# Norms of the second stream placed inside other projections, queries and keys reordered, bank halves reduced first

## What is computed

```python
# layer 2 (pool), for both streams; layer 3 (attention), queries of the latent stream only
mod = silu(c) @ ada_w[i] + ada_b[i]            # sh1, sc1, g1, sh2, sc2, g2; with c_ctx for the context
a = modulate(rms_norm(h, norm_g[i, 0]), sh1, sc1)
y = pool_mix(a, pool_w, pool_scale)            # layer 2: windowed means, then a 1024 x 256 grouped product
h = h + g1 * y
m = modulate(rms_norm(h, norm_g[i, 1]), sh2, sc2)
h = h + g2 * (square(relu(m @ mlp_w1[i])) @ mlp_w2[i])   # hidden width 4096
# layer 3
q, k, v = qkv(a_latent); kc, vc = qkv(a_context)         # 8 query heads, 4 key/value heads of 128
q, k = axial_rope(head_norm(q)), axial_rope(head_norm(k)); kc = head_norm(kc)
y_latent = attention(q, [kc, k], [vc, v]) @ w_o          # then the MLP and a last norm
```

## Time and profile before

| | us |
|---|---|
| median of 3 runs | 1587.86 |
| the profiled execution | 1588.41 |
| its span in the profile | 1585.9 |
| PE busy | 1490.0 |
| DVE busy | 1113.0 |
| ACT busy | 760.0 |

### The profile page before, as it was taken

The page is one execution under the profiler, slowest core; times in us unless marked ns, Lnnn a source line. Parts: engine busy times, 40 slices in busy tenths (PEclk is TensorE's granted clock), DMA queues, the critical chain, the costliest instruction groups (busy, mean ns, idle before and its releaser), DMA issues.

```text
span 1585.9 us, 21196 instructions
## 1 busy us (share of the span) xinstructions
PE 1490.0 (94%) x8517; PEld 1202.0 (76%) x8517; DVE 1113.0 (70%) x1682; ACT 760.0 (48%) x1184; POOL 0.2 (0%) x4
## 2 busy tenths in 40 slices
PE   5999899999999799999999999899999998899997
PEld 3767778888787568888778878688787776778786
DVE  3566758998769868998676555867767685465656
ACT  3334544444544445344465544555545534455543
POOL 0000000000000000000000000000000000000000
PEclk9999999999999899999999999899999999999999
DMA  9993158888565757776647555486674740245452
GB/s 361 343 320 136 54 186 292 293 286 304 206 239 183 243 186 260 266 245 239 213 151 274 186 186 186 161 302 233 248 255 146 269 140 27 79 133 178 172 189 86
DMA packets 167913, 335.22 MB, mean 211 GB/s; under 512 B 8192, under 2 KB 109192, under 8 KB 167816
## 3 DMA queue, kind: packets, MB, share of 16 engines
q1 hardware_dynamic: 140992, 235.09, 43.8%
q10 hardware_dynamic: 26824, 98.79, 16.8%
HBM read 332.81 MB, written 1.05 MB: 211 GB/s over the span
## 4 chain that ended last, share of the span: by engine, by line
PE 59%; DVE 25%; ACT 8%; DMA 4%; issue 4%; ACTq 0%; SPq 0%; DVEq 0%
PE ps L1860 11%; PE ps L1861 11%; PE ps L1862 11%; PE ps L1929 11%; DVE wlo L1138 9%; PE ps L1930 5%; ACT whi L659 4%; DVE hbuf L1160 3%; DMA ring<-in_ada_w_dram 3%; ACT hbuf L679 2%; PE ps L1791 1%; DVE res L1226 1%; DVE work L1224 1%; PE ps L2024 1%; PE ps L2101 1%
## 5 line engine op out<-in xcount | busy, mean ns | idle before, releaser
L1138 DVE TENSOR_TENSOR wlo<-wraw,whi 128x1024 fp32r<-128x1024 f32 (+1 forms) x420 | 493.2, 1216 | 202.9 <-ACT whi L659 202.3
L659 ACT ACTIVATE whi<-wraw 128x1024 fp32r<-128x1024 f32 (+1 forms) x420 | 418.3, 1044 | 227.0 <-PE ps L1862 139.1
L1929 PE MATMUL ps<-hT,whi 128*128 128x512 f32 x1472 | 519.4, 398 | 2.7 <-DVE hT L1281 2.7
L1930 PE MATMUL ps<-hT,wlo 128*128 128x256 f32 x1472 | 411.1, 279 | 0.0
L1929 PEld LDWEIGHTS ps<-hT,whi 128*128 128x128 f32 x1472 | 276.5, 188 | 74.0 <-DVE hT L1281 4.3
L1930 PEld LDWEIGHTS ps<-hT,wlo 128*128 128x128 f32 x1472 | 277.7, 189 | 0.0
L1860 PE MATMUL ps<-whi,act_hi 128*128 128x512 f32 x560 | 219.6, 392 | 9.0 <-DVE wlo L1138 9.0
L1862 PE MATMUL ps<-whi,act_lo 128*128 128x512 f32 x560 | 218.0, 389 | 0.0
L1861 PE MATMUL ps<-wlo,act_hi 128*128 128x512 f32 x560 | 218.0, 389 | 0.0
L1860 PE MATMUL ps<-whi,hT 128*128 128x512 f32 (+2 forms) x416 | 161.6, 388 | 4.6 <-DVE hT L1281 3.9
L1861 PE MATMUL ps<-wlo,hT 128*128 128x512 f32 (+2 forms) x416 | 158.7, 382 | 0.0
(11 more groups left out here) (230 smaller groups left out, 1398.8 us busy)
## 6 DMA issues: line engine op xcount, KB each, us to landing
wraw<-in_mlp_w_dram SPq DMA_DIRECT2D x96, 1024.0 KB, 5.3
ring<-in_ada_w_dram ACTq DMA_DIRECT2D x64, 1024.0 KB, 7.0
work<-in_ada_w_dram ACTq DMA_DIRECT2D x28, 1024.0 KB, 7.6
wraw<-in_ffn_w_gate_dram SPq DMA_DIRECT2D x22, 1024.0 KB, 5.5
wraw<-in_ffn_w_up_dram SPq DMA_DIRECT2D x22, 1024.0 KB, 6.8
wraw<-in_ffn_w_down_dram SPq DMA_DIRECT2D x22, 1024.0 KB, 5.0
wraw<-in_diff_w_in_dram SPq DMA_DIRECT2D x12, 1024.0 KB, 5.2
wraw<-in_attn_w_qkv_dram SPq DMA_DIRECT2D x12, 1024.0 KB, 5.0
```

What stands on the lines that cost most here:

```text
L659: nc.scalar.activation(whi[:, u % 2, part], raw_view(u)[:, part], ACT.Copy).then_inc(hi_ready, 1)
L1138: nc.vector.tensor_tensor(wlo[:, u % 2, part], raw_view(u)[:, part], whi[:, u % 2, part].bitcast(F32), ALU.subtract).then_inc(lo_ready, 1)
L1929: mm(ps[:, bank, :], whi[:, u % 2, c0:c0 + P], hT[:, :, k, :], start=(k == 0), stop=False, skip_group_check=True)
L1930: ins = mm(ps[:, bank, 0:S], wlo[:, u % 2, c0:c0 + P], hT_hi[:, k, :], start=False, stop=(k == KT - 1), skip_group_check=True)
```

## The change

It has five parts.

1. In DVE's stream, hidden_out(i) comes ahead of split_unit(i + 2) in every up and pair stream.
2. Norm 6 (the context's pooling norm) runs beside down20, and norm 8, which is now the latent stream's attention norm, beside down21: ACT takes squares at units 4 and 5, scales at 7 and does columns at 10 and 13, DVE does rows at 6 and columns at 10 and 14, PE its products after units 9 and 12. The columns go to other memory (spent), the pool matrices are loaded at unit 6. pool1's products then come straight after down20; the pool's gate products come after them, in banks of their own, and nine idle products stand after each pool in the place of the vector units.
3. The order of the last projections is q3, kvl, kvc. Norm 9 is the context's; its rows run beside q3, its transposes after kvl's second unit, and it is placed into hT as kvl's units let go of it. The head norms follow in the order q3, kvl, kvc, and columns(3, 1) move from attention into q3.
4. Vectors 18, 19 (both streams), 22 and 23 join 20 and 21 in SUMMED: 20 adds in up20, 12 in down20, and the same in up21 and down21. The vector units in the gaps go.
5. A product into a bank waits for that bank alone (bank_emptied); IDLE_NORM loses two entries, IDLE_HEADS[3] goes from 46 to 20.

The core of the diff:

```diff
-        IDLE_NORM = {1: 7, 2: 6, 4: 2, 8: 6, 9: 2, 10: 5}
+        IDLE_NORM = {1: 7, 2: 6, 4: 2, 10: 5}
-        IDLE_HEADS = {1: 5, 3: 46}
+        IDLE_HEADS = {1: 5, 3: 20}
+        IDLE_POOL = 9
...
-        seg("kvc", "row", [QKV[:, :, 1024:2048]], 4)
         seg("q3", "row", [QKV[:, :, 0:1024]], 4)
         seg("kvl", "row", [QKV[:, :, 1024:2048]], 4)
+        seg("kvc", "row", [QKV[:, :, 1024:2048]], 4)
...
-        VECTOR_AT = list(range(20)) + [22, 23, 20, 21]
+        VECTOR_AT = list(range(20)) + [21, 22, 20, 23]
...
+        LATE = ("up20", "down20", "up21", "down21")
+        SUM_SPANS = [(("up0", "down0"), (6, 7, 8), slots(1, 22, 24)), (("up0", "down0"), (9,), slots(22, 28, 8)),
+                     (("up1", "down1"), (15, 16), slots(1, 27, 32)), (LATE, (18, 19), slots(1, 16, 20) + slots(18, 28, 12)),
+                     (LATE, (20, 21, 22, 23), slots(33, 48, 20) + slots(50, 60, 12))]
...
         NORMS = [(0, 0, 0), (0, 0, 1), (0, 1, 0), (0, 1, 1), (0, 2, 0), (0, 2, 1), (1, 2, 0), (1, 2, 1),
-                 (1, 3, 0), (0, 3, 0), (0, 3, 1)]
+                 (0, 3, 0), (1, 3, 0), (0, 3, 1)]
+        BESIDE_DOWN = (6, 8)
...
+            def norm_beside_down(i):
+                if i == 2:
+                    root_table()
+                if i in (4, 5):
+                    norm_squares((i - 4,))
+                if i == 7:
+                    norm_scale()
+                if i == 10:
+                    norm_columns((1,))
+                if i == 13:
+                    norm_columns((3,))
...
                 for i in range(s_["count"]):
-                    if i < s_["count"] - 2:
-                        split_unit(s_["base"] + i + 2)
-                    if i == s_["count"] - 2 or i == s_["count"] - 1 and not hold_last:
+                    hidden_out(s_, i)
+                    if i < s_["count"] - 1 or not hold_last:
                         split_unit(s_["base"] + i + 2)
-                    hidden_out(s_, i)
                     row_adds(name, i)
...
+                else:
+                    held_split("down20")
+                    pool_gate(1, POOL_GATE_BANKS)
                 residual(s_)
                 norm()
                 split_unit(by_name[f"pool{s_}"]["base"] + 2)
-                stream(f"up2{s_}", beside=lambda i: vector_out(19) if s_ == 1 and i == 1 else columns(3, 0) if s_ == 1 and i == 3 else None)
-                stream(f"down2{s_}", hold_last=True)
+                stream(f"up2{s_}", beside=lambda i: columns(3, 0) if s_ == 1 and i == 5 else None)
+                stream(f"down2{s_}", hold_last=True, beside=norm_beside_down)
                 residual(s_)
...
+            row_segment("q3", heads=other_rows)
+            panel_rows(q3, 0, 1024)
+            held_split("q3")
+            row_segment("kvl", heads=other_columns)
+            panel_rows(kvl, 0, 1024)
+            norm_place(3)
+            held_split("kvl")
+            heads3(1, (3,))
+            row_segment("kvc", heads=lambda i: heads3(2, range(i, min(i + 1, 3))))
+            panel_rows(kvc, 0, 1024)
             heads3(2, (3,))
+            heads3(0, range(4))
...
+            def norm_beside_down(i):
+                if i == 9:
+                    norm((0, 1, 2))
+                if i == 12:
+                    norm((3,))
...
-                if strm == 0:
-                    vector_units(18, 0, 2)
-                else:
-                    vector_units(19, 2, 4)
+                if strm == 1:
+                    gate(POOL_GATE_BANKS)
+                idle_products(T_BANKS[6][2], IDLE_POOL)
                 gate()
                 norm()
-                up_segment(f"up2{strm}", beside=lambda i: columns(3, 0, 20) if strm == 1 and i == 2 else None)
-                down_segment(f"down2{strm}")
-
-            vector_units(22, 0, 4)
-            norm()
+                up_segment(f"up2{strm}", beside=lambda i: columns(3, 0, 20) if strm == 1 and i == 4 else None)
+                down_segment(f"down2{strm}", beside=norm_beside_down)
+
+            row_segment("q3", beside=lambda i: columns(3, 1, 24) if i == 2 else None)
+            row_segment("kvl", beside=lambda i: norm() if i == 1 else None)
+            fed[0] = (sem("hT_ready"), len(HT_STEPS) * BESIDE_ROWS, HT_STEPS)
             row_segment("kvc")
-            vector_units(23, 0, 2)
-            norm()
-            row_segment("q3")
-            row_segment("kvl")
-            vector_units(23, 2, 4)
             gate()
             idle_products(IDLE_BANK, IDLE_HEADS[3])
-            columns(3, 1, 24)
```

More of the change, by code:

```diff
@@ L435, in build @@
         PANEL_SEGS = ["in0_2", "in0_0", "in0_1", "out0", "down0", "in1_0", "in1_1", "in1_2", "out1", "down1",
-                      "pool0", "down20", "pool1", "down21", "kvc", "q3", "kvl", "out3", "down3"]
+                      "pool0", "down20", "pool1", "down21", "q3", "kvl", "kvc", "out3", "down3"]
         panel_end = [by_name[n_]["base"] + by_name[n_]["count"] for n_ in PANEL_SEGS]
@@ L698, in stream @@
                         ring_fill(fill_to)
+                    if beside is not None:
+                        beside(i)
                     if s_["kind"] == "down" and i == s_["count"] - 4:
@@ L746, in norm_rows @@
                 junk = full.rearrange("p (q a) n -> p q (a n)", q=4)
-                for t in range(TT):
+                for t in tiles:
                     for h in range(2):
@@ L1298, in norm_columns, with pool_gate @@
                     low(slice(6, 8))
+            def pool_gate(s_, banks):
+                dve.wait_ge(sem("pool_landed"), 32 * (s_ + 1))
+                for h in range(2):
+                    dve.wait_ge(gate_psum, 2 * (4 + 2 * s_) + h + 1)
+                    nc.vector.tensor_tensor(gate_b[:, 512 * h:512 * h + 512], ps[:, banks[h], :], wk(2048 + 512 * h, 512), ALU.mult).then_inc(sem("pool_gate"), 1)
             def norm():
@@ L1724, in heads3, with other_rows, other_columns @@
                     rotate(rv, acos, asin, [z[:, 0:nh * 256] for z in rot3], 32)
-            for n, (name, rows) in enumerate((("q3", q3), ("kvl", kvl))):
-                row_segment(name, heads=lambda i: heads3(n, range(i, min(i + 1, 3))))
-                panel_rows(rows, 0, 1024)
-                if name == "q3":
-                    held_split(name)
-                heads3(n, (3,))
-            heads3(2, range(3))
-            vector_out(23)
+            def other_rows(i):
+                if i == 2:
+                    norm_rows()
+                if i == 3:
+                    columns(3, 1)
+            def other_columns(i):
+                if i == 1:
+                    norm_modulate()
+                if i == 2:
+                    norm_place(0)
+                    norm_place(1)
+                if i == 3:
+                    norm_place(2)
+                else:
+                    heads3(1, (i,))
+            row_segment("q3", heads=other_rows)
+            panel_rows(q3, 0, 1024)
+            held_split("q3")
+            row_segment("kvl", heads=other_columns)
+            panel_rows(kvl, 0, 1024)
+            norm_place(3)
+            held_split("kvl")
+            heads3(1, (3,))
+            row_segment("kvc", heads=lambda i: heads3(2, range(i, min(i + 1, 3))))
+            panel_rows(kvc, 0, 1024)
             heads3(2, (3,))
+            heads3(0, range(4))
             nc.vector.memset(mark[:, 1:2], 0.0).then_inc(sem("heads3"), 1)
-            held_split("kvl")
+            held_split("kvc")
             turns(3)
-            attention(3, beside=lambda i: columns(3, 1) if i == 2 else None)
+            attention(3)
             out_turn(3)
@@ L1974, in down_segment, with norm @@
                         beside(i)
-            def norm():
-                n = norm_no[0]
-                norm_no[0] += 1
-                strm = NORMS[n][0]
+            def norm(blocks=(0, 1, 2, 3)):
+                if 0 in blocks:
+                    norm_no[0] += 1
+                n = norm_no[0] - 1
                 if n in PLAIN:
@@ L1983, in norm @@
                 mats = wk(0, 4 * TT * POOL_BAND).rearrange("p (g j n) -> p g j n", g=4, j=TT)
-                idle_products(IDLE_BANK, IDLE_NORM.get(n, 0))
-                for b in range(4):
+                if 0 in blocks:
+                    idle_products(IDLE_BANK, IDLE_NORM.get(n, 0))
+                for b in blocks:
+                    if b == 3 and n in BESIDE_DOWN:
+                        pe.wait_ge(sem("hT_ready"), len(HT_STEPS) * n + 2)
+                    if b == 3 and n == BESIDE_ROWS:
+                        bank7_wait()
                     if b % 2 == 0:
@@ L2014, in gate @@
                 idle_products(IDLE_BANK, IDLE_GATE.get(e, 0))
-                for t in range(TT):
-                    emptied(n, t)
+                if banks is D_BANKS:
+                    for t in range(TT):
+                        emptied(n, t)
                 pe.wait_ge(mod_rows, VECTOR_AT.index(6 * l + 3 * f + 2) + 1)
@@ L2271, in _ @@
```

(2 more changed lines are left out.)

205 lines of the change are left out of this document (135 added, 70 removed).

## The result

The changed kernel took 1566.69 us (median of 4 runs, 1563.57 to 1568.88) against 1587.76 for the kernel before beside it (4 runs): a ratio of 0.9865, 95% interval 0.984 to 0.9889. That is 21 us less; the forecast was 1563.4 (25 us less), the range 1556 to 1574. The profiled execution is the one of 1563.57 us.

What follows compares the result with a forecast made beforehand. The prediction took PE as the bound, with time won where it no longer waits; -14.6 + 9.8 - 9.1 - 1.4 - 9.4 - 0.3 = -25.0 took 1588.4 to 1563.4 us, range 1556 to 1574.

Steps and rivals of the forecast that it cites:

- Part 1: Up20, up21 and up3 with their first down units: reduce ahead of split brings them near PE's rate, -14.6 us.
- Part 2: More vector sums on DVE in up and down streams: no cost in time except six more pick-ups on PE, +3.6 us.
- Rival D: More sums make DVE the bound of the up streams, so the kernel gets slower, 1603 us; chance 0.04.
- Part 3: Norms beside down20 and down21: hidden on ACT and DVE; PE's added products and the pick-ups together +9.8 us.
- rival E: Norms beside the down streams stall PE for as long as they took in the gap, 1572.5 us; chance 0.04.
- Part 4: Gap around pool1, from down20 to up21: vector units, gate and norm 6 go, 30.3 to 21.2 us, -9.1.
- T: The time at which down20 ends, 996.4 us in the profile before; the gap to up21 is counted from it.
- Part 5: Gap behind pool0: the products of vector 18's first half and their wait go from before the gate, -1.4 us.
- Part 6: Queries and keys, from down21 to the head turns: new order starts turns after 94.2 us, not 103.6, -9.4.
- Rival A: The key heads' chain on DVE before the turns is as late as before, 1573 us; chance 0.11.
- B: The reorder gains nothing, since PE waits for the wlo that now comes 1.2 us later, 1578 us; chance 0.07.
- C: PE's clock falls at each new stall, 1568 us, at most 1572 with two stretches slowed; chance 0.14.

Runs made afterwards that it cites:

- e1: The changed kernel with the split put ahead of the reduce again in DVE's stream: 1575.77 us, ratio 0.9921 to the kernel before.
- e5: The changed kernel with the queries' head norm (sums, root, scaling) moved earlier, into DVE's wait behind down21: 1561.06 us, ratio 0.9842.
- e2: The kernel before with only the reduce put ahead of the split in DVE's stream: 1573.11 us, ratio 0.9913.
- e4: The changed kernel with each add of up21 issued twice on DVE, the second result unread: 1575.88 us (one run).
- e7: The changed kernel without the nine idle products behind each pool: 1564.26 us, ratio 0.9861.
- e12: The changed kernel with the pool's products waiting as before the change, in place of bank by bank: 1565.96 us (one run).
- e3: The changed kernel with unread products, transposes or waits put between up units at 15 places: 1568.91 us (one run).

## Why the prediction was right

*Part 1, the reorder (-14.6).* Right as a mechanism, shown by the relus' idle time (129.1 to 0 and back to 129.8 when undone) and by the reorder alone (-14.3 in the three stretches, two of them at 5.55 us per unit there). In the changed kernel it is worth 8.8 (e1). Where the time would come out was wrong in part: I read units of 5.81 us as what the loop costs, but only eight units of up20 were so long, and up21's and up3's ran at 5.55 and 5.65. The loop was there in all three streams, as I had reckoned it; PE paid for it at the turns, which became 10.0 us shorter together, while the up units took the same in sum. The term was mis-sized in one more place: I let up20 and up21 run at up1's 5.556 us, "near the far end, since up1's row shows that rate held". They ran at 5.65 in the profiled execution, 16 x 0.1 = 1.6 us each, which is the +1.2 and +1.3 by which those two streams missed their forecast, and a little more. What I wrote of up3 ("spaced a little wider for a reason that I don't see") was the same thing: a pattern chosen per execution, not a property of the stream.

*Part 2, the sums.* No cost in time beyond the pick-ups; these came to 9.4 - 6.0 = 3.4 us (3.6 forecast). Rival D did not come, but its margin was read too narrowly per unit; over a stretch DVE had 16 us to spare.

*Part 3, norms beside down units.* up20's and up21's down units run on without a wait (75.92 and 74.31 us with PE busy throughout), so rival E falls. PE's added work is there as reckoned.

*Part 4, the gap.* 21.24 against T + 21.2. Two errors cancelled: the second residual came 0.8 us earlier, and what follows took 0.8 us longer. The condition on which it stood, products bank by bank, was worth 6.4 us.

*Part 5.* -1.75 against -1.4; DVE waits 0.65 us for the transposes there, where it waited 2.54.

*Part 6.* -8.25 against -9.4, and in part by luck. The chain after the modulating took 51.5 us in place of 49.8, but it is not made of the terms that I added up. I counted a rotation (4.45) for the keys of both streams; those of the context have none, and behind their gain at 1292.50 comes the next split. And I left out the queries' root, their two scalings and their first gain, which stand in the chain from 1242.54 to 1246.39 and from 1250.60 to 1252.98, 6.2 us. With 1.4 us of waits on ACT and PE, which I had set to none, and the other terms 1.4 us shorter, the errors nearly cancelled.

```profile
1242.54 0.17 DVE L1444 TENSOR_SCALAR stat<-stat 128x16 f32<-128x16 f32 x1
...
1251.73 1.22 DVE L1436 TENSOR_TENSOR work<-work,gains 128x1024 f32<-128x1024 f32 x1
...
1292.50 1.41 DVE L1436 TENSOR_TENSOR work<-work,gains 128x512 f32<-128x512 f32 x2
1293.95 1.22 DVE L1216 TENSOR_TENSOR wlo<-wraw,whi 128x1024 fp32r<-128x1024 f32 x1
```

Rival A falls by the time of the stage, although its sign, a chain of more than 50 us, was there; e5 shows that this chain is the bound.

*The rivals.* B falls by e1 and e2, D by e4 for the adds as they are, E by the windows of the down units, A by the stage's row. C showed its mechanism in e7 and e12, with 1.4 us and 2.2 us, but not in the changed kernel: PEclk of the last stage is 0.96, and 0.84 in the gap, where it was 0.98 and 0.85.

In all: forecast -25.0, measured -21 and -26 in the two comparisons, -22.1 in the stages of the profile. Given the scatter of single executions (some 10 us), the stages tell the terms, and the medians only the sum.

## What to carry to other kernels

Where an engine does one job for the past unit and one for a coming one, put first the job that another engine waits for on its way to freeing the coming unit: here 1.2 us of reduce ahead of 2.4 us of split took 129 us of waits off ACT and 14 us off the time. The time came back where the lag was paid, in the first units of the next stream, and not where the waits stood. A stretch that is bound by such a loop takes added work on TensorE for nothing; once the loop is gone, the same work costs its full time, so the two changes don't add. Wait for the bank that is read, not for the panel: here the wait for four banks in place of one made the gap 6.4 us longer, some 4 by the wait and 2.2 by the clock that was lost in it (one run).

## What the runs showed that was not expected

TensorE's stream of up products (512 and 256 columns in turn) runs in one of two steady patterns at the same granted clock of 1.00: 230 + 117 ns per pair of products (5.55 us per unit), or 236 + 117 on the mean (5.65), three spacings in turn. Each execution chooses per stream at its start, and a pick-up, a transpose, a product or a wait between two units can switch it either way. With 92 up units it could be worth up to 9 us between executions of one kernel. That it makes the scatter (1556 to 1569 us) is not shown: in the two profiled executions of the changed kernel the five up streams took 526.2 and 524.7 us together, and the spans were 1561.8 and 1562.1.

A larger part of the scatter lies ahead of up0, where no variant differs from the changed kernel: in the twelve traces of it and its variants up0 begins between 230.6 (e3) and 240.4 us (e1). Of these 9.9 us 9.5 lie in one window of the first block, first of e1, then of e3, with the same 812 products in both:

```profile
90.81:212.39 121.58, 107.94 (x812) 86.00 (x808) 74.86 (x214) 55.36 (x152) 0.00 (x0) 0.89 0.38 136
90.45:202.55 112.10, 98.27 (x812) 77.47 (x808) 74.87 (x214) 55.27 (x153) 0.00 (x0) 0.98 0.42 147
```

The granted clock was 0.89 in one and 0.98 in the other. What in the engine makes the two patterns, and why the clock differs between executions there, was not found.
